# Two transformer blocks on one core: fourteen small edits to waits, fillers and the order of late work

## The chip, the cores and the metric

The kernel runs on one core of a Trainium2 chip, as one launch. The metric is device time in microseconds (us) of that core, lower is better. The core has a matrix engine (TensorE, PE in the profile; PEld is its weight load), three engines for element-wise work (VectorE or DVE, ScalarE or ACT, GpSimd or POOL) and SyncE (SP), which here only issues transfers. SBUF is the on-chip memory, PSUM the eight banks into which TensorE writes.

## The reference

Input is one sequence of 256 tokens of width 1024, in fp32. The first block has two layers, `x = x + gate * mixer(h)`, where h is the RMS norm of x, scaled and shifted, and shift, scale and gate come from a product of silu(c) with a matrix of 1024 x 3072 (adaLN).

- Layer one is an NSA mixer: 16 heads of 64, keys and values in two groups; three branches (compressed keys, selected blocks, a window) whose outputs are weighted by sigmoid gates and summed, `(o * silu(z)) @ w_out`. With 256 tokens all four blocks of the selection are taken, so that branch and the window are both causal attention.
- Layer two is a dilated mixer: three groups of heads with three dilations, each group scaled by a share computed from the softmax sums of all heads, and again `(o * silu(z)) @ w_out`.

The second block has two layers of attention (MLA with sliding-window heads, then forgetting attention with chunked heads), each with a layer norm and a SwiGLU FFN of width 2816 behind it:

```
x = layer_norm(ALPHA * x + mix)
x = layer_norm(ALPHA * x + (silu(x @ w_gate) * (x @ w_up)) @ w_down)
```

## The kernel before, in words

**Tiles.** The 256 tokens are two tiles of 128 partitions (`t` = 0, 1). Every weight matrix is cut into items, which SyncE fetches in one fixed order into a ring of two slots (`fetch`, L746); the fetch of item n waits until item n-2 has been read (`released`, L389). Each product is made of three: an item is cast to a rounded high part (`whi`, by ScalarE: `high` L1500, `high_out` L1517), VectorE subtracts it to get a low part (`wlo`: `low` L1893, `low_out` L1969), and `split_products` (L961 to 964) adds high x high, high x low and low x high in one bank. Activations are split in the same way: TensorE transposes (`turn_pe`, L485), ScalarE copies the result out as the high part (`turn_act`, L495), VectorE makes the low part (`turn_low`, L526). `dil_out`, `ab_out` and `cd_out` have their first two items split by GpSimd (`split_item`, L896 to 907) during the attention before.

**Order.** Each engine has one program, written out by hand; engines meet only in semaphores. Nothing is planned at run time.

**Attention.** `att_pe`, `att_dve` and `att_act` (L569 to 676) go over pairs of heads, p = 0, 1, ... At step p TensorE computes the scores of pair p (L579, L581), transposes the probabilities of pair p-1 (L590), runs `behind(p)`, multiplies probabilities and values of pair p-2 (L604 to L606), and runs `after(p)`. VectorE scales and masks the scores and finds the maxima (L629, L631), then takes the output of pair p-2 from PSUM (`take`) and signals `att["outs"]`, which frees the bank; ScalarE does the exponentials (L659, L660) and copies transposed probabilities to `probT` (L670). NSA has 32 jobs (16 pairs), layer two has 16.

**Work woven into the attention of NSA** (`nsa_behind` L1296, `late_copies` L1745, `woven` L2278). Late blocks: six of the eight blocks of adaLN's product that aren't needed at once (`LATE_AT`, L397). One takes two items of the ring: 16 matmuls into G[3] (`late_parts`, L407), a sum by VectorE (L418), a product with ones that spreads it to all partitions (L413), a copy by ScalarE (L423). The compressed branch: its scores (L1277), softmax, a turn (L1285) and four products (L1294, at `OUT_AT`), of which each is weighted by VectorE (L2250) and added by GpSimd (`add_compressed`). Near the end `nsa_out` items 0 and 1 are split, and the first heads are gated with silu(z) (`gate_heads`, L2266).

**Layer two.** `set_gated` (L1963) takes a pair: reciprocal (L1959), product with PSUM (L1961), and product with silu(z) in `u` (L1967). `take_shared` applies the group shares (L2371, and L1820 on ScalarE).

**Output projections.** `project_out` (L1112 on TensorE, L1604 on ScalarE, L1984 on VectorE): four groups are turned, then four items are multiplied for both tiles; VectorE adds the result to x and normalises it (`ada_norm` L1937, `norm_2` L2388), where GpSimd raises the variance to -0.5 (L838).

**FFN.** `ffn_pe` (L1068): 22 steps with `gate_up` (L1076, L1077) into banks S and T and `down` (L962 to L964) into G[0..3], two banks per tile. After it the layer norm of tile 0 starts with `tile0` (`ffn_out`, L2066), that of tile 1 when the last `used` is there.

**Fillers.** `keep_busy(n)` (L981 to 985) multiplies constants into a free bank; nothing reads the result.

## Time and profile before

| | us |
|---|---|
| median of 3 runs | 1044.71 |
| lowest, highest run | 1042.41, 1045.11 |
| the profiled execution | 1046.95 |
| its span (first to last instruction) | 1045.2 |
| TensorE busy | 991.8 (95%) |
| VectorE busy | 648.0 (62%) |
| ScalarE busy | 462.2 (44%) |
| GpSimd busy | 152.9 (15%) |

Mean granted clock of TensorE over the span is 0.978 of full speed. Matmuls are pipelined, so a TensorE that is busy for 95% is not one at its peak. Times of rows are counted from the start of the span. In a timeline, [x <-E ...] at the end of a row says that the engine stood idle for x us before the row and what ended that. The nine stages: early blocks and first projection to 104 us, NSA attention to 206, its projection and the layer-two projection to 330, layer-two attention to 370, projections to 455, MLA and sliding-window attention to 485, the first FFN to 702, the forgetting attention's block to 845, the second FFN and the norm to the end.

### The profile page before, as it was taken

Reading aid. Unit: us, or ns where it says so; the run is one execution under the profiler, and the core shown is the slowest. Engines: PE = TensorE matmul, PEld = TensorE weight load, DVE = VectorE, ACT = ScalarE, POOL = GpSimd, SP = SyncE. Lnnn points to the kernel's source line nnn. Section 1 sums busy time; section 2 is a strip of 40 time slices with the busy share of each in tenths; the row PEclk is TensorE's granted clock in tenths of the full one; section 3 lists DMA queues with packets and bytes.
Section 4 is the critical chain, followed back from the end, with each engine's and each line's share of the span. In section 5 each row is a group of like instructions: output and inputs, shape, how many; then the busy total and the mean of one; then the engine's idle time right before and its main releaser. Section 6 shows DMA issues by size and latency. Waiting matters only on the chain.

```text
span 1045.2 us, 15188 instructions
## 1 busy us (share of the span) xinstructions
PE 991.8 (95%) x5752; PEld 830.9 (79%) x5752; DVE 648.0 (62%) x1137; ACT 462.2 (44%) x713; POOL 152.9 (15%) x130
## 2 busy tenths in 40 slices
PE   5999998898999899999999999999999999999996
PEld 2899765676887678987888888878998788888885
DVE  4556564665674755756876666667446487666666
ACT  2253454533444524565334444434436344444442
POOL 3006001300890500140000000000006000000000
PEclk9999899699999989999999999999999999999998
DMA  9963356134555425321366566534533235654441
GB/s 377 364 239 137 109 193 231 72 121 161 194 179 210 162 95 211 128 82 45 118 226 237 201 209 197 190 143 150 189 129 122 79 134 187 228 197 181 181 181 40
DMA packets 23670, 178.41 MB, mean 171 GB/s; under 512 B 3743, under 2 KB 4175, under 8 KB 7111
## 3 DMA queue, kind: packets, MB, share of 16 engines
q1 hardware_dynamic: 19408, 166.70, 43.4%
q0 software_dynamic: 2224, 8.94, 3.0%
q10 hardware_dynamic: 1991, 2.14, 0.6%
q8 instruction: 30, 0.49, 0.2%
q14 instruction: 17, 0.14, 0.0%
HBM read 176.72 MB, written 1.05 MB: 170 GB/s over the span
## 4 chain that ended last, share of the span: by engine, by line
PE 86%; DVE 8%; ACT 2%; DMA 2%; issue 1%; POOL 0%; SPq 0%; DVEq 0%; ACTq 0%; POOLq 0%
PE G L962 14%; PE G L963 14%; PE G L964 14%; PE S L1077 8%; PE T L1077 7%; PE S L1076 3%; PE T L1076 3%; PE T L590 3%; PE T L485 2%; PE G L606 2%; PE G L604 2%; PE G L605 2%; PE G L407 1%; DVE wlo L1902 1%; PE G L985 1%
## 5 line engine op out<-in xcount | busy, mean ns | idle before, releaser
L2024 DVE TENSOR_TENSOR wlo<-ring,whi 128x2048 fp32r<-128x2048 f32 x88 | 154.4, 1758 | 88.8 <-ACT whi L1646 52.9
L962 PE MATMUL G<-whi,hTh 128*128 128x512 f32 (+3 forms) x560 | 198.8, 355 | 4.2 <-DVE hTl L526 2.8
L963 PE MATMUL G<-wlo,hTh 128*128 128x512 f32 (+3 forms) x544 | 186.8, 343 | 0.0
L964 PE MATMUL G<-whi,hTl 128*128 128x308 f32 (+3 forms) x496 | 167.4, 337 | 0.0
L1902 DVE TENSOR_TENSOR wlo<-ring,whi 128x1024 fp32r<-128x1024 f32 (+3 forms) x76 | 120.9, 1629 | 72.5 <-ACT whi L1513 72.2
L1077 PE MATMUL S<-hT,whi 128*128 128x512 f32 x336 | 122.0, 397 | 0.0
L962 PEld LDWEIGHTS G<-whi,hTh 128*128 128x128 f32 x560 | 105.8, 189 | 19.2 <-DVE hTl L526 5.7
L1077 PE MATMUL T<-hT,whi 128*128 128x512 f32 x336 | 120.7, 394 | 0.0
L1513 ACT CAST whi<-ring 128x1024 fp32r<-128x1024 f32 (+3 forms) x76 | 87.8, 1205 | 56.7 <-PE G L964 32.2
L963 PEld LDWEIGHTS G<-wlo,hTh 128*128 128x128 f32 x544 | 102.8, 189 | 9.1 <-issue 1.8
L964 PEld LDWEIGHTS G<-whi,hTl 128*128 128x128 f32 x496 | 93.3, 188 | 5.7
L1641 ACT CAST whi<-ring 128x2048 fp32r<-128x2048 f32 x44 | 83.9, 1906 | 27.4 <-PE S L1147 17.6
L1076 PE MATMUL S<-hT,wlo 128*128 128x256 f32 x294 | 82.6, 281 | 0.0
L1076 PE MATMUL T<-hT,wlo 128*128 128x256 f32 x294 | 81.4, 277 | 0.0
L1651 ACT ACTIVATE sil<-gsum 128x256 f32<-128x256 f32 x44 | 18.4, 418 | 132.8 <-DVE gsum L2045 132.8
L1077 PEld LDWEIGHTS S<-hT,whi 128*128 128x128 f32 x336 | 63.1, 188 | 13.6 <-DVE wlo L2024 0.3
L838 POOL TENSOR_TENSOR rstd<-var,mhalf 128x1 f32<-128x1 f32 x18 | 9.9, 554 | 425.7 <-DVE var L1914 316.0
L1077 PEld LDWEIGHTS T<-hT,whi 128*128 128x128 f32 x336 | 63.0, 188 | 11.0
L962 PE MATMUL G<-whi,acth 128*128 128x512 f32 x176 | 68.6, 390 | 0.0
L964 PE MATMUL G<-whi,actl 128*128 128x512 f32 x176 | 68.5, 389 | 0.0
L963 PE MATMUL G<-wlo,acth 128*128 128x512 f32 x176 | 68.5, 389 | 0.0
L1646 ACT CAST whi<-ring 128x1024 fp32r<-128x1024 f32 x44 | 46.2, 1050 | 28.9 <-PE G L964 28.9
(356 smaller groups left out, 1829.0 us busy)
## 6 DMA issues: line engine op xcount, KB each, us to landing
ring<-in_ffn SPq DMA_DIRECT2D x44, 1536.0 KB, 6.4
ring<-in_ada_w SPq DMA_DIRECT2D x16, 1024.0 KB, 6.5
ring<-in_dil_w_in SPq DMA_DIRECT2D x16, 1024.0 KB, 4.8
ring<-in_cd_w_in SPq DMA_DIRECT2D x10, 1232.0 KB, 5.4
ring<-in_nsa_w_in SPq DMA_DIRECT2D x8, 1432.0 KB, 11.1
early<-in_ada_w SPq DMA_DIRECT2D x8, 1024.0 KB, 17.1
ring<-in_ab_w_in SPq DMA_DIRECT2D x4, 1440.0 KB, 6.6
vec<-in_vecs POOLq DMA_DIRECT2D x11, 512.0 KB, 5.2
```

Source lines behind the costliest of these rows:

```text
L485: ins = pe.transpose(turn_bank(name, g)[0:width, n * P:(n + 1) * P], src, ident)
L590: ins = pe.transpose(TB[j % 2][:, b * P:(b + 1) * P], scr[:, j % 4, 1 + b * P:1 + (b + 1) * P], ident)
L962: pe.matmul(out_, act_h, w_h, start=first_, stop=False)
L963: pe.matmul(out_, act_h, w_l, start=False, stop=False)
L964: return pe.matmul(out_, act_l, w_h, start=False, stop=last_)
L1076: pe.matmul(bank[:, 0:T], wlo[b][:, at], hT2[:, k, 0, :], start=False, stop=False)
L1077: ins = pe.matmul(bank[:], whi[b][:, at], hT2[:, k, :, :].rearrange("p h t -> p (h t)"), start=(k == 0), stop=(k == KT - 1))
L1513: sc_e.copy(whi[(k0 + j) % 2][:, at], raw[:, at]).then_inc(hi_done, 1)
L1641: sc_e.copy(whi[b][:, gu], ring[:, b, gu]).then_inc(st["gu_hi"], 1)
L1646: sc_e.copy(whi[b][:, dn], ring[:, b, dn]).then_inc(st["dn_hi"], 1)
L1902: TT(wlo[k % 2][:, at], raw[:, at], whi[k % 2][:, at].bitcast(F32), ALU.subtract).then_inc(lo_done, 1)
L2024: TT(wlo[b][:, part], ring[:, b, part], whi[b][:, part].bitcast(F32), ALU.subtract).then_inc(st[what + "_lo"], 1)
```

## The change

It makes no change to what is computed. Its parts, in the order of time:

1. The last filler call after early block 2 is left out (`if b != 2`); one is added behind the turn `nsa_rot`; four behind layer two's attention become two.
2. `LATE_AT` goes from (2, 5, 7, 9, 11, 12) to (2, 4, 7, 9, 11, 13), `OUT_AT` from (6, 8, 10, 13) to (6, 8, 10, 12); the turn of the compressed probabilities goes from pair 4 to 5; GpSimd adds the last compressed product one branch earlier.
3. Item 0 of `nsa_out` is cast in quarters, between the exponentials of heads 29 to 31 and behind pair 15, instead of at once behind pair 13; item 1 is cast and subtracted behind the turn of pair 16 instead of behind pair 15.
4. `ada_norm` and `norm_2` of tile 1 send the variance to GpSimd before other work of VectorE instead of after it.
5. A dummy Exp on ScalarE stands before the turn of layer two.
6. `set_gated` becomes a reciprocal and four `scalar_tensor_tensor` of 64 columns, each reading PSUM, the reciprocal and silu(z).
7. The turn `ab_c` uses four banks instead of two.
8. The last steps of both FFNs are taken out of the loop; three of step 20's four banks come first, then tile 0 of step 21, then the rest.

```diff
@@ -394,7 +394,7 @@
-        OUT_AT, LATE_AT, LATE_DIL = (6, 8, 10, 13), (2, 5, 7, 9, 11, 12), (-1, 2)
+        OUT_AT, LATE_AT, LATE_DIL = (6, 8, 10, 12), (2, 4, 7, 9, 11, 13), (-1, 2)
@@ -463,7 +463,7 @@
                 return (TB[0], TB[1], S[1], TB[1])[g]
-            return (S + TB)[g] if name in ("o0", "o1", "o2", "o3") else TB[g % 2]
+            return (S + TB)[g] if name in ("o0", "o1", "o2", "o3", "ab_c") else TB[g % 2]
@@ -659,7 +659,7 @@
                                         scale=-1.0).then_inc(att["probs"], 1)
-                    if between is not None:
+                    if between is not None and i < n:
@@ -886,10 +886,10 @@
             add_compressed(2)
-            for q in range(1, 4):
+            for q in range(1, 3):
...
             add_compressed(3)
-            for q in range(4, H // 2):
+            for q in range(3, H // 2):
@@ -1079,29 +1079,34 @@
-                def down(b, s, start, stop):
+                def down(b, s, stop, banks=((0, 0), (0, 1), (1, 0), (1, 1))):
...
                     pe.wait_ge(st["act_ready"], s + 1)
-                    for t in range(NT):
-                        for half in range(2):
-                            at = slice(2 * KT * P + half * 512, 2 * KT * P + (half + 1) * 512)
-                            ts = slice(t * P, (t + 1) * P)
-                            ins = split_products(G[2 * t + half][:], acth[:, b, ts], actl[:, b, ts], whi[b][:, at], wlo[b][:, at], start, stop)
-                        if t == 0 and stop:
-                            ins.then_inc(st["tile0"], 1)
-                    ins.then_inc(used, 1)
+                    for t, half in banks:
+                        at = slice(2 * KT * P + half * 512, 2 * KT * P + (half + 1) * 512)
+                        ts = slice(t * P, (t + 1) * P)
+                        ins = split_products(G[2 * t + half][:], acth[:, b, ts], actl[:, b, ts], whi[b][:, at], wlo[b][:, at], False, stop)
+                    return ins
...
                 gate_up(1, 1)
-                down(0, 0, False, False)
-                with pe.Fori(0, (FF_STEPS - 2) // 2) as i:
+                down(0, 0, False).then_inc(used, 1)
+                with pe.Fori(0, (FF_STEPS - 4) // 2) as i:
...
                         gate_up(j, s + 1)
-                        down(1 - j, s, False, False)
-                down((FF_STEPS - 1) % 2, FF_STEPS - 1, False, True)
+                        down(1 - j, s, False).then_inc(used, 1)
+                pe.wait_ge(st["hidden"], FF_STEPS - 3)
+                gate_up(0, FF_STEPS - 2)
+                down(1, FF_STEPS - 3, False).then_inc(used, 1)
+                pe.wait_ge(st["hidden"], FF_STEPS - 2)
+                gate_up(1, FF_STEPS - 1)
+                down(0, FF_STEPS - 2, False, ((0, 0), (0, 1), (1, 0)))
+                down(1, FF_STEPS - 1, True, ((0, 0), (0, 1))).then_inc(st["tile0"], 1)
+                down(0, FF_STEPS - 2, False, ((1, 1),)).then_inc(used, 1)
+                down(1, FF_STEPS - 1, True, ((1, 0), (1, 1))).then_inc(used, 1)
@@ -1197,7 +1202,8 @@
                         turn_pe(pe, "h0", only=2 * (b // 2) + t)
-                keep_busy(4, S[(b + 1) % 2], ident)
+                if b != 2:
+                    keep_busy(4, S[(b + 1) % 2], ident)
@@ -1254,6 +1260,7 @@
             turn_pe(pe, "nsa_rot", queries_ready)
+            keep_busy(1, G[1])
@@ -1299,8 +1306,8 @@
                     compressed_scores()
-                elif p == 4:
-                    pe.wait_ge(late["taken"], 1)
+                elif p == 5:
+                    pe.wait_ge(late["taken"], 2)
@@ -1309,10 +1316,9 @@
                         pe.wait_ge(nsa_s["cmp_sub"], 1)
-                    elif p == 5:
-                        pe.wait_ge(nsa_s["cmp_taken"], 1)
                     else:
-                        pe.wait_ge(nsa_s["cmp_summed"], sum(at < p for at in OUT_AT))
+                        if p > OUT_AT[0]:
+                            pe.wait_ge(nsa_s["cmp_summed"], sum(at < p for at in OUT_AT))
@@ -1395,7 +1401,7 @@
             att_pe(pe, "dil", dil_behind, dil_after)
-            keep_busy(4, G[3])
+            keep_busy(2, G[3])
@@ -1747,20 +1753,35 @@
                     sc_e.activation(sc[:], sc[:], ACT.Exp).then_inc(nsa_s["cmp_exp"], 1)
-                if p == 4:
+                if p == 5:
...
                     late_take(sc_e, LATE_AT.index(p), G[3])
-                if p == 13:
-                    high_out("nsa_out", 0)
                 if p == 15:
-                    high_out("nsa_out", 1)
+                    high_quarter(3)
...
-            att_act(sc_e, "nsa", behind=late_copies)
+                    high_out("nsa_out", 1)
...
+            def high_quarter(quarter):
...
+                n, w = first["nsa_out"], OUT_K * OUT_W // 4
+                if quarter == 0:
+                    sc_e.wait_ge(landed[n % 2], 16 * (n // 2 + 1))
+                    sc_e.wait_ge(used, split0["nsa_out"] - 1)
+                at = slice(quarter * w, (quarter + 1) * w)
+                ins = sc_e.copy(whi[0][:, at], ring[:, n % 2, at])
+                if quarter == 3:
+                    ins.then_inc(hi_done, 1)
...
+            def item_quarters(i):
...
+                if i >= 2 * H - 3:
+                    high_quarter(i - (2 * H - 3))
...
+            att_act(sc_e, "nsa", between=item_quarters, behind=late_copies)
@@ -1800,6 +1821,7 @@
                 dil_take(DIL_C - 1, t, (DIL_C - 1) % 2, True)
+            sc_e.activation(gate[:, 0, 0:1], gate[:, 0, 0:1], ACT.Exp)
@@ -1936,8 +1958,11 @@
+                if t == 1:
+                    squared_var(0, t)
                 done(TT(tok[:, t, :], x[:, t, :], mod[:, D:2 * D], ALU.mult))
-                squared_var(0, t)
+                if t == 0:
+                    squared_var(0, t)
@@ -1962,9 +1987,14 @@
-                set_pair(p, o, summed, r)
-                cols = slice(2 * p * DH, (2 * p + 2) * DH)
-                done(TT(tok[:, :, cols], tok[:, :, cols], u[:, :, 3 * D + 2 * p * DH:3 * D + (2 * p + 2) * DH], ALU.mult), sig)
+                done(dve.reciprocal(r.unsqueeze(3), summed))
+                for t in (1, 0):
+                    for j in range(2):
+                        at = (2 * p + j) * DH
+                        ins = STT(tok[:, t, at:at + DH], o[:, j, t, :], r[:, j, t:t + 1], u[:, t, 3 * D + at:3 * D + at + DH], ALU.mult, ALU.mult)
+                    if t == 1 and sig is not None:
+                        ins.then_inc(sig, 1)
+                done(ins, att["outs"])
@@ -2293,12 +2323,12 @@
                     low_out("nsa_out", 0)
-                    low_out("nsa_out", 1, (0,))
...
                     turn_low(dve, "o0", only=1)
+                    low_out("nsa_out", 1, (0,))
@@ -2388,8 +2418,10 @@
                 if t == 1:
-                    low("ab_in", 0, 1, KT * AB_W)
+                    low("ab_in", 0, 1, KT * AB_W, (0,))
                 squared_var(1, t)
+                if t == 1:
+                    low("ab_in", 0, 1, KT * AB_W, (1,))
```

## Rows read from the trace of the kernel before

**Rows 1.** the page, part 4: shares of the chain that ended last, by engine

```profile
PE 86%; DVE 8%; ACT 2%; DMA 2%; issue 1%; POOL 0%; SPq 0%; DVEq 0%; ACTq 0%; POOLq 0%
```

**Rows 2.** windows: us, then busy us (x count) of PE, PEld, DVE, ACT, POOL; granted clock, DMA share, GB/s

```profile
119.40:126.30 6.90, 6.90 (x36) 5.54 (x39) 3.63 (x14) 2.54 (x8) 0.00 (x0) 0.51 0.01 2
180.90:187.70 6.80, 6.80 (x28) 4.64 (x28) 2.38 (x11) 0.99 (x3) 0.72 (x1) 0.51 0.48 172
198.00:211.60 13.60, 11.74 (x48) 10.17 (x48) 9.70 (x17) 7.45 (x13) 5.38 (x3) 0.50 0.23 78
365.20:372.00 6.80, 6.00 (x21) 4.26 (x20) 3.96 (x17) 1.07 (x2) 0.00 (x0) 0.51 0.01 2
```

**Rows 3.** the chain that ended last, 28 to 45 us: start us, us, what

```profile
32.68 0.89 PE S L985 x8
```

**Rows 4.** the chain at 111.98 us, and TensorE's timeline at 137 us

```profile
111.98 0.83 issue
...
137.03 0.40 PE L1285 MATMUL G<-tab,kT 128*120 128x128 f32 x2 [2.04 <-DVE kT L2242]
```

**Rows 5.** TensorE's timeline: first scores of pairs 10, 12, 14; the second late half

```profile
164.36 0.38 PE L579 MATMUL S<-kT,qT 64*128 64x128 f32 x2
...
174.15 0.38 PE L579 MATMUL S<-kT,qT 64*128 64x128 f32 x2
...
179.61 0.64 PE L407 MATMUL G<-ring,cb 128*32 128x512 f32 x4 [2.44 <-DMA ring<-in_ada_w]
...
190.04 0.38 PE L579 MATMUL S<-kT,qT 64*128 64x128 f32 x2
```

**Rows 6.** timelines of TensorE and ScalarE at the end of the NSA attention

```profile
196.31 0.41 PE L590 MATMUL T<-tab,scr 128*128 128x128 f32 x2 [2.40 <-ACT probT L670]
...
199.82 1.05 ACT L1528 CAST whi<-ring 128x1024 fp32r<-128x1024 f32 x1
```

**Rows 7.** VectorE's timeline in ada_norm of tile 1

```profile
241.88 1.28 DVE L1942 SCALAR_TENSOR_TENSOR tok<-tok,rstd,bias 128x1024 f32<-128x1024 f32 x1 [0.75 <-POOL rstd L838]
```

**Rows 8.** ScalarE's timeline at the start of the layer-two attention

```profile
334.00 1.28 ACT L659 ACT_TABLE_LOAD   x1
335.29 0.40 ACT L659 ACTIVATE scr<-scr,negmax 128x128 f32<-128x128 f32 x1
```

**Rows 9.** timelines of GpSimd, VectorE and TensorE in and behind layer two

```profile
350.93 2.35 POOL L906 TENSOR_TENSOR wlo<-ring,whi 128x1024 fp32r<-128x1024 f32 x1
...
351.78 1.78 DVE L1967 TENSOR_TENSOR tok<-tok,u 128x256 f32<-128x256 f32 x1
...
352.67 0.30 PE L590 MATMUL T<-tab,scr 128*128 128x128 f32 x1 [1.39 <-ACT probT L670]
...
353.81 0.42 DVE L631 CUSTOM_DVE_ANT_0 scr<-G,tab 128x256 f32<-128x256 f32 x1
...
363.49 0.30 PE L590 MATMUL T<-tab,scr 128*128 128x128 f32 x1 [1.43 <-ACT probT L670]
...
446.25 0.29 DVE L535 TENSOR_TENSOR tmp<-u,tab 128x128 f32<-128x128 f32 x1 [2.41 <-ACT u L1626]
446.46 0.29 DVE L536 TENSOR_TENSOR tmp<-u,tab 128x128 f32<-128x128 f32 x1
```

**Rows 10.** timelines of TensorE and ScalarE at the end of layer two's attention

```profile
369.29 5.07 PE L985 MATMUL G<-tab 128*128 128x512 f32 x8
...
370.79 1.07 ACT L1820 ACTIVATE tok<-tok,glse 128x384 f32<-128x384 f32 x2 [5.76 <-DVE glse L2366]
```

**Rows 11.** TensorE's timeline in the turn ab_c

```profile
434.43 0.44 PE L485 MATMUL T<-tab,tok 128*128 128x128 f32 x2 [1.36 <-DVE cTl L526]
```

**Rows 12.** timelines of VectorE and TensorE at the end of the second FFN

```profile
1031.37 0.43 DVE L2054 TENSOR_TENSOR actl<-act,acth 128x256 fp32r<-128x256 f32 x1 [0.47 <-ACT acth L1656]
...
1032.27 0.39 PE L962 MATMUL G<-whi,acth 128*128 128x512 f32 x1
```

**Rows 13.** the page, part 6: DMA issues, KB each, median us to landing

```profile
ring<-in_nsa_w_in SPq DMA_DIRECT2D x8, 1432.0 KB, 11.1
```

## The prediction

> **What bounds the kernel now.** I read the chain that ended last first: TensorE carries 86% of it, VectorE 8%, ScalarE 2%, DMA 2% [rows 1]. So a part of the change is worth what TensorE stands still for it, or what TensorE does at its lower clock because of it. The next view was the granted clock of four stretches [rows 2]: TensorE is at 1.2 GHz (a mean of 0.50 to 0.51) for 34.1 us, all of it in or just after attention stages, and in the last two of these its work has holes (11.74 us busy of 13.60, 6.00 of 6.80). The rest of the span stands at 2.4 GHz. Then I read the timeline around each place that the diff touches, taking only the wait that ends last there. The long projections and FFN loops show hardly a wait, so nothing can be won in them; what they start later or earlier, they end later or earlier.
>
> **The change, part by part** (times on the clock of the profiled execution; a gain is time that leaves TensorE's chain).
>
> Start. Four filler calls after early block 2 go. The chain holds 0.89 us of them directly before the products of block 3 [rows 3], which then start without a wait for their raw part. Gain 0.9; 0 if that part lands only at the end of the fillers.
>
> First turn of NSA. One filler call (two matmuls, 0.86 us at full clock) enters a hole of 0.83 us [rows 4]: no cost. Whether it spares the low stretch from 119.4 to 126.3 is open. That stretch has light work ahead of it too, 32 matmuls of 30 columns, which stay. Bounds: 0, and 2.7, if the TensorE work between 117.6 and 129.3 runs at full clock. I take 0, since the light work is nearer to the fall than the filler is.
>
> Turn of the compressed probabilities moved from pair 4 to 5, late block 1 from 5 to 4. Now TensorE stands 2.04 us for VectorE's probabilities [rows 4]. After, the block's 16 matmuls (1.85 us) fill that; its sum on VectorE comes after two scores of pair 4 (136.9 + 1.4 + 0.7 = 139.0), the broadcast matmuls end at 140.0, and with the turn (0.5) and the usual 3.0 pair 6 starts at 143.5, where it starts at 144.8 now. Gain 1.3 (0.5 to 2.0).
>
> Last late block from pair 12 to 13, last compressed product from 13 to 12. Both halves of the block are fetched when ring slots fall free; the second arrives at 179.6 and holds TensorE for 2.44 us [rows 5], and the low clock of 180.9 follows. Pairs 10 and 11 have the content that 12 and 13 get: 9.79 us (164.36 to 174.15) against 15.89 (174.15 to 190.04). After, that second half is wanted near 180.8, when it has landed. Gain 6.1; at least 2.4, the wait alone. VectorE's scale of the modulation at head 28 waits for this block, which now ends as pair 14 starts: about 0.1 late, nothing.
>
> Item 0 in quarters. One cast of 2048 columns (1.90 us) behind pair 13 becomes four of 512 (0.55 each, an estimate from 1.05 for 1024 [rows 6]) among the exponentials of heads 29 to 31. Three of them stand ahead of copies for which TensorE already waits (2.40 us [rows 6]): 0.55 at pair 14 and 1.1 at pair 15 and 16, a loss. Item 1 moves behind the turn on ScalarE and VectorE: its casts (2.1) leave the path of the last copies of probabilities, and 1.75 us of subtraction no longer stand ahead of the turn. Its DMA order stays, but the fetch of item 0 now starts when late block 5 is read, about 3.5 us later. Worked through to the third turn of the projection, 24.2 us after pair 14 starts against 24.1 now, if the clock is low as now; 20.6 if it is full. The hole that lowers it is no shorter, so I take 0 (from -1.1 to +3.5).
>
> ada_norm and norm_2, tile 1. VectorE idles 0.75 us for GpSimd's power in the first [rows 7], and as long in the second; the multiplication (1.22) and half a subtraction (1.6) now cover it. Gain 0.65 each, 1.3 together; TensorE waits for that result both times.
>
> Table of Exp. The load (1.28 us) stands directly ahead of the first exponential [rows 8]. Bounds 0 and 1.28; the maxima that the exponential needs come only some 0.25 us before the load ends. The dummy Exp puts the load into the hole before the turn. Gain 0.2. The Trainium skill ("ScalarE: Activation LUTs", What ACT_TABLE_LOAD costs) adds a drain of some 1380 ns to every switch, by which the gain would be some 1.6; here the exponential follows the load at once, so the measurement decides.
>
> Gate of layer two. The product of tok and u, both in SBUF, takes 1.78 us where GpSimd splits weights (0.42 alone), while an operation on PSUM and a table in SBUF takes 0.42 in the same microseconds [rows 9]. Four scalar_tensor_tensor that read PSUM take the place of both products. Bounds of one: 0.14 us (two products of 128 columns without a wait start 0.21 apart, 0.29 long [rows 9]; 64 columns fewer take 0.07 off) and 0.42 (a whole product of 256 columns). I take 0.2, near the unwaited pair: 0.8 for four against 0.42 + 0.04 + 0.42 alone and 2.2 beside GpSimd. The waits of TensorE in four pairs, 1.39, 0.57, 0.57 and 1.43 (the first and the last stand in [rows 9]), add up to 3.96 and go. What then ends last is TensorE's own 2.95 us a pair. The last product of probabilities comes 0.4 later, since the bank is released after all four operations; if the clock stays full it takes 1.3 instead of the 2.6 up to 369.29, since it lies in the last low stretch [rows 2]. The four filler calls last to 374.36 while ScalarE has its first shared columns ready at 371.86 [rows 10], so two calls (1.7) release the turn 2.4 earlier. Together 3.96 - 0.4 + 1.3 + 2.4 = 7.3; 5.0 with the clock low; 1.4 if the stalls stay too. The Trainium skill ("VectorE: DVE Perf Modes", The DRAIN you can't avoid) says that the next operation waits until the pipe is empty, and to keep the number of operations small, which speaks against four for two; by it a take would cost some 0.3 us more and the sum would be about a microsecond smaller. The unwaited pair above contradicts it.
>
> Banks of ab_c. The third turn waits 1.36 us for a bank [rows 11]; four banks remove that, of which VectorE's next subtraction gives back 0.3. Gain 1.1.
>
> End of both FFNs. The last low activations are ready at 1031.80, the fourth bank of step 20 ends at 1032.27 [rows 12]; with three banks first, step 21 starts at 1031.87. Gain 0.4 for tile 0 and the VectorE chain behind it, twice: 0.8. TensorE itself ends 0.3 later, under VectorE's work on tile 0.
>
> Sum: 0.9 + 0 + 1.3 + 6.1 + 0 + 1.3 + 0.2 + 7.3 + 1.1 + 0.8 = 19.0. The profiled execution took 1046.95 us (span 1045.2), so 1028.0; it is 2.2 above the median shown, 1044.71, from which the sum would give 1025.7. I take the middle, 1027.
>
> **The rivals.** (A) The clock holds in NSA too: the filler and the missing stall spare the stretches at 119 and 198. For it: both follow places where a hole shrinks. Against: the hole of 2.40 us behind VectorE's scale stays [rows 6]. It gives 2.7 + 3.5 more, 1021. (B) The clock is low after all where I have it full: 2.9 of the 6.1 and 2.3 of the 7.3 are lost, 1032. For it: no wait there is the only hole. (C) The four operations are slowed by GpSimd as the product is, since u still lies in SBUF. The row with the table speaks against it. Of the 7.3 only 1.4 is left: 1033. (D) The last late block comes too late for what is behind it: item 0 is fetched at about 180.6, its first quarter is wanted at 188.2, and ScalarE would hold exponentials and copies behind it. A landing time of 11.1 us, the median of the items of nsa_w_in [rows 13] and the longest of the ring, would cost 3.5: 1030.5. (E) Slower: the clock pays for the thinned fillers. If a stretch like the one from 198.0, 13.6 us at half clock, comes up at 32, 181 and 366, each costs 6.8 against full clock, 20.4 in all, and 2.3 of the layer-two gain goes as well: 1050. It decides from about three such stretches, since two leave 1043. Against it: at 32 real products follow at once, and at 366 the stalls that led to the low clock are the ones removed.
>
> **How the numbers follow.** My case 0.50, A 0.17, B 0.15, C 0.08, D 0.07, E 0.03. The prediction is 1027. The range goes from A against the lower base (1019.5) to C with 3 us of what I took for certain failing (1036). A measurement of this kernel tells about 0.3% (3.1 us) from no change; all cases but E are over that, and for several failing at once I leave 0.03: faster 0.94, same 0.03, slower 0.03.
>
> **What would show it.** In the changed profile: no DMA wait of a late block near 175; full clock from 175 to 190; layer-two pairs 2.95 us apart with GpSimd busy; each of the four operations under 0.3 us; L485 of the third turn without a wait in ab_c; no idle VectorE ahead of the two second tiles. Products in the gating of layer two that last over a microsecond, quarters that wait for their item, or a low clock in dense work would make me wrong.

## The result and the profile after

The changed kernel took 1028.62 us (median of 4 runs, 1025.27 to 1030.22), the kernel before 1044.91 beside it (1042.41 to 1046.86): a ratio of 0.9841, 95% interval 0.9806 to 0.9876. Run again in a later set it took 1026.31 (1025.70 to 1027.58), ratio 0.9810 (0.9768 to 0.9852). The prediction was 1027.0, range 1019.5 to 1036, and faster by over 0.3% at 0.94. The profiled execution took 1030.04 us, its span is 1028.2, so 17.0 of span against the 19.0 of the sum. Three of the sum's terms were too large, one stage gained what the sum had at nothing, and a part of the time turned out to be decided anew by each execution.

The shares of the chain that ended last have hardly moved, against [rows 1] (part 4 of the page of after):

```profile
PE 87%; DVE 7%; ACT 2%; DMA 2%; issue 1%; POOL 0%; SPq 0%; DVEq 0%; ACTq 0%; POOLq 0%
```

The useful reading is the lead, the time of an instruction before minus that of the same instruction after. Where it rises, a part pays.

| instruction on TensorE | before | after | lead | by the sum |
|---|---|---|---|---|
| first scores of NSA | 112.81 | 112.11 | 0.70 | 0.9 |
| scores of pair 6 | 144.78 | 142.55 | 2.23 | 2.2 |
| scores of pair 12 | 174.15 | 172.00 | 2.15 | 2.2 |
| scores of pair 14 | 190.04 | 181.79 | 8.25 | 8.3 |
| third turn of projection one | 213.98 | 203.37 | 10.61 | 8.3 |
| turn of tile 1 behind ada_norm | 243.22 | 232.40 | 10.82 | 8.95 |
| first scores of layer two | 333.33 | 322.44 | 10.89 | 8.95 |
| third turn of projection two | 379.25 | 362.43 | 16.82 | 16.45 |
| turn of tile 1 behind norm_2 | 408.87 | 391.89 | 16.98 | 17.1 |
| products behind ab_c | 451.03 | 432.73 | 18.30 | 18.2 |
| third turn of projection three | 491.11 | 474.13 | 16.98 | 18.2 |
| turn behind FFN one | 715.79 | 699.17 | 16.62 | 18.6 |
| end of the span | 1045.2 | 1028.2 | 17.0 | 19.0 |

TensorE's timeline of after, pairs 4 to 6 and 12 to 14:

```profile
138.11 1.13 PE L413 MATMUL G<-mod,ones 128*128 128x512 f32 x2 [0.45 <-DVE mod L418]
...
140.73 0.60 PE L1292 MATMUL G<-tab,kT 128*120 128x128 f32 x4
...
142.55 0.49 PE L579 MATMUL S<-kT,qT 64*128 64x128 f32 x4
...
172.00 0.49 PE L579 MATMUL S<-kT,qT 64*128 64x128 f32 x4
...
177.54 1.92 PE L407 MATMUL G<-ring,cb 128*32 128x512 f32 x16
181.79 0.49 PE L579 MATMUL S<-kT,qT 64*128 64x128 f32 x4
```

The turn (L1292) no longer waits 2.04 us [rows 4]. The 16 products of the last late block (L407) stand in one piece of 1.92 us, where their second half waited 2.44 [rows 5]; pairs 12 and 13 take 9.79 us instead of 15.89.

Windows of after; columns as in [rows 2]:

```profile
119.90:126.70 6.80, 6.80 (x37) 3.70 (x36) 3.32 (x12) 3.46 (x10) 0.00 (x0) 0.51 0.01 2
172.00:188.00 16.00, 14.50 (x115) 10.02 (x114) 10.34 (x43) 8.50 (x21) 5.17 (x5) 1.00 0.57 229
191.00:202.00 11.00, 10.01 (x47) 8.51 (x48) 8.08 (x12) 6.59 (x9) 2.55 (x3) 0.69 0.30 97
356.00:366.00 10.00, 8.46 (x44) 6.45 (x43) 5.49 (x12) 4.62 (x7) 0.00 (x0) 1.00 0.00 1
467.00:473.00 6.00, 5.57 (x22) 4.25 (x23) 2.58 (x7) 0.67 (x1) 0.00 (x0) 0.72 0.00 0
802.00:806.00 4.00, 4.00 (x13) 2.65 (x12) 0.89 (x3) 0.00 (x0) 0.00 (x0) 0.58 0.00 0
```

The filler at 111 changed nothing in the stretch at 120. The stretches at 181 and 365 are gone, the 13.6 us from 198 [rows 2] have become two of 3.4, and there is a new one at 468 (0.72 over 6 us), where before had full clock.

TensorE and VectorE in the last pairs of NSA, after:

```profile
183.40 1.22 DVE L1952 SCALAR_TENSOR_TENSOR bias<-bias,vec 128x1024 f32<-128x1024 f32 x1
187.16 0.90 PE L590 MATMUL T<-tab,scr 128*128 128x128 f32 x6 [1.50 <-ACT probT L670]
191.06 1.05 PE L590 MATMUL T<-tab,scr 128*128 128x128 f32 x6 [1.72 <-ACT probT L670]
```

The scale of the modulation before, beside GpSimd's last compressed addition:

```profile
191.94 1.27 POOL L877 TENSOR_TENSOR tok<-tok,tmp 128x512 f32<-128x512 f32 x1
192.31 1.98 DVE L1930 SCALAR_TENSOR_TENSOR bias<-bias,vec 128x1024 f32<-128x1024 f32 x1
```

That addition now comes a branch earlier, the scale takes 1.22, and the wait of 2.40 [rows 6] is 1.50.

ada_norm and norm_2 of tile 1, after (VectorE and GpSimd):

```profile
229.30 1.23 DVE L1963 TENSOR_TENSOR tok<-x,bias 128x1024 f32<-128x1024 f32 x1
229.35 1.59 POOL L838 TENSOR_TENSOR rstd<-var,mhalf 128x1 f32<-128x1 f32 x1 [10.30 <-DVE var L1957]
231.06 1.28 DVE L1967 SCALAR_TENSOR_TENSOR tok<-tok,rstd,bias 128x1024 f32<-128x1024 f32 x1 [0.53 <-POOL rstd L838]
...
388.44 1.66 DVE L1924 TENSOR_TENSOR wlo<-ring,whi 128x1440 fp32r<-128x1440 f32 x1
388.49 2.02 POOL L838 TENSOR_TENSOR rstd<-var,mhalf 128x1 f32<-128x1 f32 x1 [10.46 <-DVE var L1957]
390.55 1.29 DVE L2426 SCALAR_TENSOR_TENSOR x<-x,rstd,vec 128x1024 f32<-128x1024 f32 x1 [0.45 <-POOL rstd L838]
```

The power of one column takes 0.56 us at the median of its 18 executions here (least 0.55) and 1.59 and 2.02 here, beside the work that was to hide it. VectorE still waits 0.53 and 0.45, where it waited 0.75 [rows 7].

Layer two, after: the gating beside GpSimd's splitting, then the start of the projection.

```profile
339.80 0.86 DVE L1994 SCALAR_TENSOR_TENSOR tok<-G,rden,u 128x64 f32<-128x64 f32 x4
339.93 2.37 POOL L906 TENSOR_TENSOR wlo<-ring,whi 128x1024 fp32r<-128x1024 f32 x1
...
349.38 0.90 PE L590 MATMUL T<-tab,scr 128*128 128x128 f32 x6 [0.77 <-ACT probT L670]
...
356.76 1.09 PE L485 MATMUL S<-tab,tok 128*128 128x128 f32 x8 [0.64 <-ACT tok L1842]
357.25 0.56 ACT L1842 ACTIVATE tok<-tok,glse 128x320 f32<-128x320 f32 x1 [0.54 <-DVE tok L1994]
...
359.62 0.47 PE L962 MATMUL G<-whi,hTh 128*128 128x512 f32 x1 [0.90 <-DVE oTl L526]
```

The four operations take 0.86 us in all with GpSimd in a subtraction of 2.37, so 0.2 each, where the product of two SBUF operands took 1.78 [rows 9]. The pairs stand 2.95 to 3.06 us apart. Of TensorE's four waits one is left, 0.77 us ahead of the last transposes, where it was 1.43 [rows 9]. The turn at 356.76 waits 0.64 for ScalarE's shares, and the first product 0.90, since ScalarE scales the third group (L1842, which needs the last gating) ahead of the turn's copies.

### The profile page after: what moved, and what is told of

Same layout as the page of the kernel before. It is cut to its first block, busy times and chain, and to the rows that moved or that the text cites. A ratio compares the mean times of both kernels' runs of the same rounds, so it can differ in the third digit from the quotient of the medians.

```text
span 1028.2 us, 15183 instructions
## 1 busy us (share of the span) xinstructions
PE 983.3 (96%) x5742; PEld 823.5 (80%) x5742; DVE 641.0 (62%) x1153; ACT 462.9 (45%) x717; POOL 153.0 (15%) x130
## 4 chain that ended last, share of the span: by engine, by line
PE 87%; DVE 7%; ACT 2%; DMA 2%; issue 1%; POOL 0%; SPq 0%; DVEq 0%; ACTq 0%; POOLq 0%
PE G L962 14%; PE G L963 14%; PE G L964 14%; PE S L1077 7%; PE T L1077 7%; PE S L1076 3%; PE T L1076 3%; PE T L590 3%; PE T L485 2%; PE G L604 2%; PE G L606 2%; PE G L605 2%; PE G L407 1%; DVE wlo L1924 1%; DMA early<-in_ada_w 1%
## 5 line engine op out<-in xcount | busy, mean ns | idle before, releaser
L838 POOL TENSOR_TENSOR rstd<-var,mhalf 128x1 f32<-128x1 f32 x18 | 12.5, 695 | 415.6 <-DVE var L1936 315.6
```

## The experiments

Each is the changed kernel with one edit, unless it says otherwise. Ratios are against the kernel before; e1 to e3 were one set, then e5 to e8, then e9 to e12, each set on one chip. The median of the changed kernel is 1028.62 before the first set and 1026.31 in the second (e5); the third has none. There is no result for e4, in which VectorE was to take the power -0.5 itself. "Third turn" is that of the projection named, on TensorE's timeline.

**Old gating of layer two** (e1)

```diff
...
-                for t in (1, 0):
...
+                set_pair(p, o, summed, r)
+                cols = slice(2 * p * DH, (2 * p + 2) * DH)
+                done(TT(tok[:, :, cols], tok[:, :, cols], u[:, :, 3 * D + 2 * p * DH:3 * D + (2 * p + 2) * DH], ALU.mult), sig)
```

> The changed kernel with the old gating of layer two put back (product with PSUM, then the product of tok and u, both in SBUF); the fillers and all else stay as changed. Theory (the slowed product was what TensorE waited for): the product takes 1.5 us or more in the pairs in which GpSimd splits weights and 0.42 in the others, TensorE stands 3 to 4 us in all between layer-two pairs again, the low clock after 365 is back, and the kernel is 4 to 7 us slower than the changed one: 1033 to 1036 us. Rival (what layer two gained came from the two filler calls and from the clock, not from the gating): at most 2 us slower, 1029 to 1031. A pair whose product ends after the scores, but without a wait of TensorE, would speak for the rival.

Measured: 1030.52 us (1028.67 to 1031.87), ratio 0.9846 (0.9827 to 0.9864). VectorE, GpSimd and TensorE:

```profile
340.03 2.35 POOL L906 TENSOR_TENSOR wlo<-ring,whi 128x1024 fp32r<-128x1024 f32 x1
340.87 1.79 DVE L1992 TENSOR_TENSOR tok<-tok,u 128x256 f32<-128x256 f32 x1
341.76 0.90 PE L590 MATMUL T<-tab,scr 128*128 128x128 f32 x6 [1.34 <-ACT probT L670]
...
352.60 0.90 PE L590 MATMUL T<-tab,scr 128*128 128x128 f32 x6 [1.43 <-ACT probT L670]
```

The four waits are back (1.34, 0.57, 0.58, 1.43), the last transposes come 3.22 us later and the third turn 2.84 (365.27 against 362.43). The clock stayed at 1.00 from 346 to 378. So the stall half of the theory holds, and the clock half does not in this execution: the same stalls did not bring the low stretch. The total, 1.9 us over the changed kernel and 2.66 over e3 in its own set, lies where the rival had it, although the rival's mechanism fell, since the waits are there.

**Old order of late blocks and turns** (e2)

```diff
-        OUT_AT, LATE_AT, LATE_DIL = (6, 8, 10, 12), (2, 4, 7, 9, 11, 13), (-1, 2)
+        OUT_AT, LATE_AT, LATE_DIL = (6, 8, 10, 13), (2, 5, 7, 9, 11, 12), (-1, 2)
```
with the compressed turn at pair 4 and GpSimd's additions in the old order.

> The changed kernel with the old order of late blocks, compressed turn and compressed products (and GpSimd's additions in the old order). Theory (each late block must come where its ring half has landed, and the compressed turn where VectorE is done): pair 6 starts 1.3 to 1.5 us later and pair 14 a further 6 us later, with a DMA wait of about 2.4 us near 175 and a low clock after 180; VectorE's scale at head 28 takes about 2 us beside GpSimd's last addition, instead of 1.22, which costs TensorE 0.8 more. In all 7.5 to 10 us slower than the changed kernel: 1036 to 1038.5. Rival (the late item is fetched when a slot falls free, so the wait only moves): under 3 us slower, 1029 to 1031.5.

Measured: 1034.74 us (1033.95 to 1035.03), ratio 0.9889 (0.9873 to 0.9906), 6.9 us over e3 in the same set. Windows and timelines of TensorE, VectorE and GpSimd:

```profile
130.00:150.00 20.00, 17.96 (x117) 12.13 (x118) 10.46 (x47) 9.08 (x24) 0.00 (x0) 0.83 0.38 140
...
181.26 1.07 PE L407 MATMUL G<-ring,cb 128*32 128x512 f32 x8 [1.30 <-DMA ring<-in_ada_w]
...
190.37 1.27 POOL L877 TENSOR_TENSOR tok<-tok,tmp 128x512 f32<-128x512 f32 x1
190.73 1.99 DVE L1954 SCALAR_TENSOR_TENSOR bias<-bias,vec 128x1024 f32<-128x1024 f32 x1
```

The total lies between the two expected ranges, and the time is lost in other places than the theory has it. Behind the turn's wait of 2.04 us the clock fell for 6.8 us, and pair 6 came 4.98 us later, not 1.3 to 1.5. Having come so late, TensorE waited only 0.27 and 1.30 for the halves of the last late block, and pairs 12 and 13 took 11.56 us: the fetch sets the time there, and a delay ahead of it is partly swallowed. The scale beside GpSimd's addition takes 1.99, as the theory says. But TensorE's next wait is 2.93 us instead of 1.50, so 1.4 more and not 0.8: VectorE's weighting of the last compressed product (0.69 us at 189.44) stands in the same pair again, ahead of the scale.

**No quarters** (e3), and item 1 cast and subtracted ahead of the turn again

```diff
+                if p == 13:
+                    high_out("nsa_out", 0)
                 if p == 15:
-                    high_quarter(3)
+                    high_out("nsa_out", 1)
...
```

> The changed kernel with items 0 and 1 of nsa_out cast and subtracted in the old way (item 0 as one cast of 2048 columns behind pair 13, item 1 before the turn). Theory P (the quarters are worth nothing; the 2.4 us that the end of NSA gained came from VectorE's scale, which no longer runs beside GpSimd's addition): the third turn of the projection of layer one comes within 1 us of where the changed kernel has it (203.4), total 1028 to 1030. Rival Q (the quarters and item 1 behind the turn brought it): the turn comes 2 to 4 us later, total 1030.5 to 1033, with a cast of about 1.9 us ahead of the last copies of probabilities and 1.75 us of subtraction ahead of the turn.

Measured: 1027.86 us (1023.86 to 1029.50), ratio 0.9813 (0.9788 to 0.9839). From the scores of pair 14 to the third turn it takes 22.13 us (181.36 to 203.49) against 21.58 changed, with a mean clock of 0.85 instead of 0.90 over 184 to 218. The executions e10 and e11, which have the quarters and the same mean clock of 0.85, take 21.31 and 21.47. So the quarters and the later item 1 are worth 0.5 to 0.8 us: the third turn is where theory P has it, within 1 us of 203.4, but "nothing" is too little. The scale takes 1.22 here too.

**The changed kernel again** (e5), no edit.

> The changed kernel itself once more, to see how far two executions of one kernel lie apart, stage by stage. Theory (the low clock comes by chance at holes, and one stretch of 3.4 us costs 1.4 to 1.7): the instructions keep their durations and the waits for VectorE and ScalarE theirs within 0.1 us, but one or two of the low stretches (191 to 201, 468, 803) are absent or elsewhere, and the span differs from 1028.2 by a multiple of about 1.5 us. Rival (the clock is fixed by the work): the same stretches in the same places, and the span within 0.5 us of 1028.2. Median 1027 to 1030 by both.

Measured: 1026.31 us, ratio 0.9810; the span is 1025.8, 2.4 less. Windows:

```profile
191.00:202.00 11.00, 9.87 (x52) 8.36 (x52) 8.09 (x12) 6.45 (x9) 2.54 (x2) 0.84 0.28 97
...
802.00:806.00 4.00, 4.00 (x20) 3.11 (x19) 0.42 (x1) 0.12 (x1) 0.00 (x0) 1.00 0.00 0
```

The pairs of NSA start within 0.2 us of each other in the two executions, and the two waits at the end are 1.50 and 1.72 in both. One of the two stretches behind 191 and that at 803 are absent, that at 468 is there. The clock is thus not fixed by the program: the same work runs at either level. What a stretch costs depends on what ends last: from the last products of probabilities of the forgetting attention to the third turn behind them it is 6.69 us with the stretch at 803 and 5.04 without (1.65), but the stretch at 198 moved the third turn by 0.17 only, since TensorE waits 1.30 us there for VectorE's gating when the clock is full. Another 0.6 of the 2.4 us lies in the first FFN, where the profile of after waits 0.43 us behind an item that landed late.

**VectorE's scale later** (e6)

```diff
-                if i == 2 * H - 4:
-                    dve.wait_ge(late["taken"], LATE_NSA)
-                    scale_gain(mod1)
...
                 evict(0, 0, 0)
+                if i == 0:
+                    scale_gain(mod1)
```

> The changed kernel with VectorE's scale of the modulation (1.22 us at 183.40) taken out of NSA's last pairs and put into VectorE's idle time of 2.23 us before its second product of the projection's results. Theory (the scale is what the wait of 1.50 us at 187.16 is made of): that wait falls to 0.3 to 0.6, pair 15's transposes come 1.0 to 1.2 us earlier, and the third turn of the projection 1 us earlier if the clock is the same; the scale in its new place costs nothing. Total 1026 to 1028. Rival (ScalarE's casts of the quarters are due at the same moment and end last): less than 0.4 us is gained at the transposes, 1028 to 1029.

Measured: 1027.34 us (1027.22 to 1027.93), ratio 0.9822 (0.9780 to 0.9863). TensorE:

```profile
185.74 0.89 PE L590 MATMUL T<-tab,scr 128*128 128x128 f32 x6 [0.38 <-ACT probT L670]
190.39 0.89 PE L590 MATMUL T<-tab,scr 128*128 128x128 f32 x6 [2.48 <-ACT probT L670]
```

The wait I aimed at fell to 0.38, and the next grew from 1.72 to 2.48; the third turn came at 203.85 with the clock at 0.85. Neither theory had the place right. By the timeline the second wait is made by VectorE's gating of eight heads, which stands ahead of the last pair's scores, and by ScalarE's quarters.

**Fillers in the two holes** (e7, and e12 for the profile)

```diff
+                if name == "nsa" and p > H - 2 and p < H + 1:
+                    pe.wait_ge(att["maxes"], 2 * (b0 + 2 * (H - 1)))
+                    pe.matmul(SB[0][0][:, 0:512], ident, tab[:, 0:512], start=True, stop=True)
```

> The changed kernel with one filler product of 512 columns (about 0.9 us) put into each of the two holes of 1.50 and 1.72 us ahead of the last two transposes of NSA. Theory (the holes are what lowers the clock from 191 to 201): both holes shrink to 0.6 to 0.9, at least one of the two low stretches goes, and the third turn comes 1.5 to 3.4 us earlier; 1025.5 to 1027.5. Rival (the fillers change nothing in the clock, it falls here whatever fills the holes): the two stretches stay, the turn comes within 0.5 us of 203.4, 1028 to 1029.5.

> The kernel with a filler in each of the two holes at the end of NSA once more, for its profile. Its median in the runs before was 0.6 us under that of the changed kernel in the same set. Theory (the holes lower the clock): no low stretch, or one instead of two, between 190 and 202, third turn at 200 to 202. Rival: stretches as in the two profiles of the changed kernel, third turn at 203.1 to 203.6.

Measured: 1025.75 us in the first set (the changed kernel there: 1026.31), ratio 0.9804 (0.9762 to 0.9846), and 1025.18 in the second. TensorE in e12:

```profile
187.39 0.90 PE L593 MATMUL T<-tab,scr 128*128 128x128 f32 x6 [0.44 <-ACT probT L673]
...
191.29 0.89 PE L593 MATMUL T<-tab,scr 128*128 128x128 f32 x6 [0.80 <-ACT probT L673]
...
201.78 0.66 PE L485 MATMUL T<-tab,tok 128*128 128x128 f32 x4 [1.30 <-DVE tok L2302]
```

The holes are 0.44 and 0.80, where e5 has 1.50 and 1.72. The clock is 1.00 from 184 to 218, the only one of ten profiles with the new turns in which it is, and the third turn comes 16.81 us behind the last scores instead of 18.46 to 18.63. All of that gain lies behind the last transposes (10.49 us to the third turn instead of 12.13 and 12.31), where after and e5 have the stretch at 191. This favours the theory, but it is one profile, and the medians of e7 and e5 differ by 0.6 us only.

**The new gating alone, in the kernel before** (e8)

```diff
-                set_pair(p, o, summed, r)
...
+                for t in (1, 0):
+                    for j in range(2):
+                        at = (2 * p + j) * DH
+                        ins = STT(tok[:, t, at:at + DH], o[:, j, t, :], r[:, j, t:t + 1], u[:, t, 3 * D + at:3 * D + at + DH], ALU.mult, ALU.mult)
...
```

> The kernel before with the new gating of layer two alone (four operations that read PSUM instead of two products); four filler calls, old turns and all else as before. Theory (the stalls of 3.96 us behind the slowed product go, and 0.4 comes back at the last take; the clock and the fillers are a matter apart): the last transposes of layer two come 3.2 us earlier against pair 0, the third turn of its projection 2.8 to 4.5 us earlier (the fillers move along with the pairs), each of the four operations starts about 0.2 after the one before, total 2.8 to 4.5 us below the kernel before, ratio 0.9957 to 0.9973. Rival (the four filler calls set the start of the turn, so nothing gets through without their halving): under 1 us gained, ratio over 0.999.

Measured: 1041.81 us, ratio 0.9957 (0.9926 to 0.9987). From the first scores of layer two to the third turn: 41.94 us (339.07 to 381.01) against 45.92, so 3.98 less, inside the theory's 2.8 to 4.5; the clock is low for 3.4 us behind the attention here. Its profiled execution took as long as one of before, 1047.27: NSA lost what layer two gained, with a clock of 0.83 over 130 to 150 and 0.66 over 184 to 218.

**The end of NSA in another order** (e9)

```diff
-                if i == 2 * H - 4:
-                    dve.wait_ge(late["taken"], LATE_NSA)
-                    scale_gain(mod1)
+                if i == 2 * H - 1:
...
+                    gate_heads(0, 8, out_ready)
...
                 if p == 15:
+                    high_quarter(2)
                     high_quarter(3)
```
with the scale as in e6, and the waits of the gating moved with it.

> The changed kernel with the end of NSA put in another order: VectorE's scale of the modulation goes into the projection (as in the run with the scale alone), its gating of the first eight heads (1.22 us at 186.09) comes behind the last pair's scores instead of ahead of them, and ScalarE does two of the four quarters of item 0 behind the copies of pair 14. Theory (the hole ahead of the last transposes, 1.72 us, and 2.48 with the scale moved, is made of the work that VectorE and ScalarE do ahead of the last pair's scores and exponentials; taking the scale away alone only moved the wait): the last transposes start near 188.5 instead of 191.06, both holes are under 1 us, the turn of heads 0 to 7 starts 2 us earlier or more, and the third turn 1.5 to 4 us earlier than in the changed kernel (203.1 to 203.4), at most one low stretch: 1023.5 to 1025.5. Rival (the projection waits for the split of item 0, or for the second item's DMA, whose slot is freed by it, and not for the transposes): the third turn within 1 us of 203.2, 1026 to 1027.5.

Measured: 1023.99 us (1022.70 to 1025.07), ratio 0.9808 (0.9784 to 0.9832). TensorE:

```profile
184.60 0.90 PE L590 MATMUL T<-tab,scr 128*128 128x128 f32 x6 [0.37 <-ACT probT L670]
187.55 0.89 PE L590 MATMUL T<-tab,scr 128*128 128x128 f32 x6 [0.77 <-ACT probT L670]
188.28 1.04 PE L485 MATMUL S<-tab,tok 128*128 128x128 f32 x8
192.02 0.44 PE L604 MATMUL G<-u,probT 128*128 128x65 f32 x2 [1.42 <-DVE tmp L2298]
```

Both holes are small, and the turn comes 4.97 us behind the last scores instead of 7.11 to 7.16. A new wait of 1.42 takes a part of that back (the bank of the last products, behind VectorE's subtraction of 2.29 us), and the third turn is 1.4 to 1.6 us nearer than changed, 17.03 behind the last scores, with a mean clock of 0.90 over 184 to 218. Not all of the lower median is the edit's: in the profiles of e9, e10 and e13 the low stretch at 120 lasts 3.4 us instead of 6.8, and the scores of pair 14 come 68.0 us behind those of pair 0 instead of 69.7, though nothing ahead of them differs from the changed kernel, nor from e12, which ran on the chip of e9 and e10 and has 6.8.

**The cover cut in two** (e10)

```diff
-                done(TT(tok[:, t, :], x[:, t, :], mod[:, D:2 * D], ALU.mult))
+                for half in range(1 + t):
+                    at = slice(half * D // (1 + t), (half + 1) * D // (1 + t))
+                    done(TT(tok[:, t, at], x[:, t, at], mod[:, D + at.start:D + at.stop], ALU.mult))
```
and the half subtraction of norm_2 in two pieces of 720 columns.

> The changed kernel with the VectorE work that is to hide GpSimd's power cut in two: the product of x and scale in two halves of 512 columns (0.69 each instead of 1.23), and the half subtraction in norm_2 in two pieces of 720 columns. Theory (GpSimd's small operation does not run until the VectorE operation in flight has ended, since both use SBUF through one port): the power in ada_norm is done 0.5 us earlier (about 1.1 instead of 1.59 long), that in norm_2 about 0.8 earlier, VectorE no longer waits for it, and the turn of the second tile comes 0.2 to 0.4 us earlier in each of the two stages; total no more than 0.8 us less, 1026 to 1028. Rival (GpSimd is slowed in proportion, for as long as VectorE has two operands in SBUF): the power takes 1.6 and 2.0 us as before, the waits of 0.53 and 0.45 stay less the 0.15 that the extra operation costs, and nothing is gained.

Measured: 1025.28 us (1023.82 to 1026.69), ratio 0.9829 (0.9805 to 0.9853). VectorE and GpSimd:

```profile
227.68 1.42 DVE L1965 TENSOR_TENSOR tok<-x,bias 128x512 f32<-128x512 f32 x2
227.72 1.06 POOL L838 TENSOR_TENSOR rstd<-var,mhalf 128x1 f32<-128x1 f32 x1 [10.31 <-DVE var L1957]
229.13 1.29 DVE L1969 SCALAR_TENSOR_TENSOR tok<-tok,rstd,bias 128x1024 f32<-128x1024 f32 x1
...
386.63 1.73 DVE L2430 TENSOR_TENSOR wlo<-ring,whi 128x720 fp32r<-128x720 f32 x2
386.67 1.27 POOL L838 TENSOR_TENSOR rstd<-var,mhalf 128x1 f32<-128x1 f32 x1 [10.46 <-DVE var L1957]
```

The power takes 1.06 and 1.27 us: one of VectorE's two operations (half of 1.42 and of 1.73) and 0.35 to 0.40 more. Uncut it was 1.23 and 1.66, and the power 1.59 and 2.02, so 0.36 more. GpSimd's operation is held until VectorE's ends, not slowed in proportion. VectorE waits no more, and from variance to result it is 1.63 instead of 1.94 us and 1.82 instead of 2.29. TensorE's turns of the second tiles come 0.3 and 0.46 us nearer to the third turns ahead of them (28.72 instead of 29.03, 29.00 instead of 29.46), so this is the wait that ends last there. The Trainium skill ("Trainium Architecture — The Big Picture", What this means for kernel authors) says that VectorE and GpSimd share a pair of ports and that this is an exclusive lock, not a split of the bandwidth; these rows agree.

The rows of before show the same in the other direction, where GpSimd started first. VectorE's scale ends 1.08 us behind the end of GpSimd's addition (1.22 alone; the same 1.08 in e2), and the product of tok and u ends 0.28 to 0.29 behind the end of GpSimd's subtraction in all four pairs (0.42 alone). So VectorE's operation too is held, until 0.14 us before GpSimd's ends, and then takes its usual time: the 1.78 us of [rows 9] are not a slower product but a wait for the rest of a GpSimd operation of 2.35 us.

**Old fillers** (e11)

```diff
-                if b != 2:
-                    keep_busy(4, S[(b + 1) % 2], ident)
+                keep_busy(4, S[(b + 1) % 2], ident)
...
-            keep_busy(1, G[1])
...
-            keep_busy(2, G[3])
+            keep_busy(4, G[3])
```

> The changed kernel with the old filler calls (four after early block 2, none behind nsa_rot, four after layer two). Theory (fillers beyond a wait are plain cost; they don't hold the clock): the third early block's products 0.7 us later, pair 0 of NSA 0.7 later, the low stretch at 120 as it is; in layer two two calls more (0.43 each product, 1.7 in all) against a wait of 0.64 that they fill: the turn 1.0 to 1.2 us later. Total 1.7 to 2 us slower, 1028 to 1030. Rival (fillers hold the clock in what follows): the turn later by as much, but low stretches at 191 to 201 or 468 absent, total within 1 us of 1026 to 1028. A third way, that the clock falls at 366 again when four calls run there, would show 2.5 us or more at the third turn of layer two.

Measured: 1030.01 us (1028.41 to 1031.49), ratio 0.9867 (0.9841 to 0.9893). TensorE:

```profile
354.70 5.35 PE L985 MATMUL G<-tab 128*128 128x512 f32 x8
359.89 1.04 PE L485 MATMUL S<-tab,tok 128*128 128x128 f32 x8
```

Pair 0 of NSA starts 0.64 to 0.75 later, the low stretch at 120 is as it was. In layer two the turn comes 10.0 us behind the last transposes instead of 7.38: 2.6 more, over the 1.0 to 1.2 of the theory and as the third way has it, since the four calls run in a low stretch (5.35 us for 8). The clock stretches at 190 and 470 are there. Fillers in this place are plain cost, and nothing shows that they hold the clock. The whole is 4.7 us over e10, of which e10's own edit is 0.8; the traces account for some 3 of the rest.

**Together** (e13): e9, e10, and the filler of projection one moved into the hole of 1.42 us.

```diff
+                elif p == H + 1:
+                    pe.wait_ge(late["taken"], LATE_NSA)
+                    keep_busy(1, G[3])
...
-                keep_busy(1, G[3])
+                if i != 0:
+                    keep_busy(1, G[3])
```

> What the runs so far point to, together: the reordered end of NSA (scale and gating later, two quarters behind the copies), the split work over GpSimd's power, and the filler of the first projection moved from behind the last products of probabilities, where it stands 1 to 2 us in TensorE's way, into the hole of 1.42 us ahead of them. Theory (the parts are independent, and a hole with a filler in it costs nothing): the waits ahead of the last transposes stay at 0.4 and 0.8, the third turn of the first projection comes another 1 to 2.5 us earlier than 17.0 us behind the scores of the last pair, the second tiles gain 0.3 and 0.45; 1020.5 to 1023.5, ratio 0.977 to 0.9805. Rival (the products of item 0 then wait for VectorE's low parts instead, so nothing of the filler is won): third turn 16.5 to 17.5 behind those scores, 1023 to 1025.

Measured: 1024.76 us (1024.01 to 1025.56, 6 runs), ratio 0.9792 (0.9763 to 0.9821). TensorE:

```profile
198.70 0.66 PE L485 MATMUL T<-tab,tok 128*128 128x128 f32 x4 [1.98 <-DVE tok L2309]
```

The third turn comes 15.2 us behind the last scores, 1.8 nearer than in e9 and as the theory has it, but it waits 1.98 for the gating of the last heads and a low stretch follows: the fourth turn is at 203.53 in both kernels. The total is where the rival has it, by another mechanism than the rival's: the wait moved on to VectorE's last gating. The ratios of e9 (0.9808) and of this version (0.9792) stand against 0.9841 and 0.9810 of the changed kernel, and the intervals overlap: that either beats it is not shown.

## Why the prediction was right, and where its steps were not

**Held.** Fillers at the start: 0.86 for 0.9 at their own place (from the first products at 27.64 to the filler at 35.35 it is 7.71 us before and in e11, 6.85 after); the lead shows 0.70, because the execution of after ran 0.17 us late ahead of it. The filler behind nsa_rot: 0, and the stretch at 120 stays. Turn and late block 1: 1.5 for 1.3. Late block 5: 6.1 for 6.1, though e2 shows that it isn't a constant: pairs 12 and 13 of the old order took 15.89, 17.26 (e8) and 11.56 us (e2) against 9.79. Table of Exp: 0.22 for 0.2. Banks of ab_c: the wait of 1.36 [rows 11] is gone, 1.3 for 1.1. Rival C fell, and with it the microsecond that the drain rule would have cost: four operations in 0.86 us beside GpSimd. The rule was cited by half: the same section of the Trainium skill ("VectorE: DVE Perf Modes", The DRAIN you can't avoid) says that an operation which is not held starts earlier, and the four start some 0.2 us apart. D fell: the last late block's products stand in one piece, and no quarter waits for its item. E fell. Of A half came true, 6.8 us of low clock behind 191 instead of 13.6. B did not show in the profile of after, but a stretch of 3.4 us lies behind layer two's attention in e3, e6, e10, e11 and e12, so it is a matter of the execution.

**The step that failed: "the multiplication (1.22) and half a subtraction (1.6) now cover it. Gain 0.65 each".** It gained 0.21 and 0.15 for the 1.3. I had used the contention with GpSimd in one direction (VectorE's product at 1.78) and not in the other. Both operands of the covering work lie in SBUF, so GpSimd's power stands still until it ends (e10).

**The step that was mis-sized: the gate of layer two, 7.3.** It was 5.7 (lead 10.89 to 16.82, less 0.2 for the table). The first wrong part is "add up to 3.96 and go": 3.0 went, since a wait of 0.77 us stays ahead of the last transposes; e1 and e8 put the stalls at 3.2 and with the clock at 3.98. The second is "what then ends last is TensorE's own", which overlooked ScalarE's share of the third group: from the turn to the third turn it is 5.67 us instead of 5.05, 0.6 lost. The other two parts came out as summed: 1.0 for 0.9 between the last transposes and the fillers (the clock less the later bank), and 2.3 for the fillers' 2.4 (2.6 in e11). But that the clock belongs to the gate ("1.3 instead of 2.6") is not borne out: e1 has all four stalls and full clock, e8 has none and a low stretch.

**Also mis-sized: the ends of the FFNs, 0.4 each.** From the last low activations to tile 0's statistics it is 2.33 us in both, against 2.57 and 2.56 before, so 0.24 each: TensorE, now early, waits 0.19 for the activations, and tile 0's products still take their time. In the second step of the first FFN an item landed late in the profile of after (ScalarE waits 2.05 us for it instead of 1.51), which took 0.5 of the lead.

**The end of NSA, "I take 0".** It gained 2.4. I had said of VectorE's scale only that it starts late. Left out was that the same edit moves two things away from it: GpSimd's addition (0.77 us) and VectorE's own weighting of the last compressed product (0.69). From the scores of pair 14 to the third turn, at the same mean clock of 0.85, it is 22.91 us with the old order (e2), 22.13 without the quarters (e3), and 21.31 and 21.47 with both (e10, e11). By these four executions some 1.5 us are the new place of the last compressed product, and 0.7 to 0.8 the quarters with the later item 1. That leaves some 0.2 of the 2.4 for the clock, although the low clock there is 6.8 us instead of 13.6; two such single profiles can differ by as much.

**A reading that was wrong: "The rest of the span stands at 2.4 GHz".** The kernel before is also at half clock for 3.4 us near 820 (0.57 over 819 to 823). No term hangs on it; the stretch at 803 after stands at the same point of the program.

**What the sum had no term for.** The low stretch at 468 costs 1.65 us (the lead falls by 1.32 only, since a wait of 0.33 us that before has at 473.13 is gone): from the turn to the third turn of projection three it takes 10.0 us with it (after, e5) and 8.35 without (e3, e6, e12). No part of the change touches that stage; the stretch is there in five of the ten profiles with the new turns (after, e1, e5, e9, e11) and in none of the three with the old ones. Nor had the prediction a term for how far executions differ. The mean granted clock of three windows, from the profiles (windows view), tells it:

| | 130 to 150 | 184 to 218 | 346 to 378 |
|---|---|---|---|
| before | 1.00 | 0.74 | 0.89 |
| e8 (old turns) | 0.83 | 0.66 | 0.95 |
| e2 (old turns) | 0.83 | 0.85 | 0.95 |
| after | 1.00 | 0.90 | 1.00 |
| e5, the same kernel | 1.00 | 0.95 | 1.00 |
| e1 | 1.00 | 0.95 | 1.00 |
| e3, e6, e10, e11 | 1.00 | 0.85 | 0.95 |
| e9 | 1.00 | 0.90 | 1.00 |
| e12 | 1.00 | 1.00 | 0.95 |
| e13 | 1.00 | 0.95 | 0.89 |

With the old turns two of three profiles are low behind the hole of 2.04 us at 137; with the new turns none of ten. Two of the three also lie under all others behind 184. This speaks for the moved turns being worth more than the waits that they remove, since they take away holes behind which the clock may fall; but three profiles against ten are few. Over all sets the kernel before ran between 1040.47 and 1053.21 us, the changed one between 1025.27 and 1030.22. That its spread is smaller for this reason is my reading; that the clock differs between executions of the same instructions is shown by e5, and on one chip by e9, e10 and e12.

**Luck in the number.** The sum was 19.0 and the profile gives 17.0, with errors of both signs. The two power terms, the gate and the FFN ends were 2.9 us too large together, the stretch at 468 and the late item took another 1.8, and the end of NSA gave back 2.4 that the sum did not have. Without that offset the sum would have been 4 us off, so that the forecast lies so near is in part luck.

What stays open: why the clock falls behind one hole of an execution and not behind the same hole of the next, and whether e12's full clock is the fillers' doing. Nor is there a measurement of a power taken by VectorE itself (e4).

## What to carry to other kernels

Take a wait for GpSimd as hidden only under VectorE work that has at most one operand in SBUF, or cut that work in pieces: the small operation runs when the piece in flight ends. The second way was run for the power (e10). For the first there are only rows of before: GpSimd's addition of 256 columns takes 0.73 us beside a product of VectorE that reads PSUM (at 191.13), 0.72 at the least elsewhere, and 1.70 beside one with two operands in SBUF (at 195.87). Where a wait is taken out of the last items of a chain, name the next one before counting the gain: at the end of NSA it moved three times (e6, e9, e13). Credit an edit with stalls, and keep what the clock gives in the range: one profile can't tell it from chance, so profile the same kernel twice before explaining a stretch.

## What was unexpected about the hardware

- One program and the same holes to 0.1 us: the granted clock fell behind them in one execution and not in the other (stretches of 3.4 us at 198 and 803; the first moved the third turn by 0.17 us, the second by 1.65). The two executions may be of two chips; but on one chip the low stretch at 120 lasts 3.4 us in e9 and e10 and 6.8 in e12, with the same instructions up to there.
- A GpSimd operation on a single column takes 0.55 us alone, 1.06 to 2.02 beside a VectorE operation on two SBUF operands, by the length of that operation and 0.35 to 0.40.
- A VectorE operation of 1024 columns with two SBUF operands takes 1.22 us alone and 1.98 and 1.99 beside GpSimd's addition of 512 columns (1.27) that started before it: it ends 1.08 us behind that addition's end, so it is held and not slowed.
- Four scalar_tensor_tensor of 64 columns that read PSUM, the reciprocal and one SBUF table take 0.86 us, with GpSimd busy or not.
